# State and output stage of a gated linear attention layer: updates in four row groups, states scaled on ScalarE, low parts on VectorE

## The reference, cut to what matters

```python
b = jnp.cumsum(g, axis=1)
o_inter = q*exp(b) @ S
A = (q k^T with decay exp(b_t - b_s), lower triangle)
o_intra = A @ v
k_dec = k * exp(b_last - b)
S_new = exp(b_last)[..., None] * S + k_dec^T @ v
...
o = o * rsqrt(mean(o*o) + EPS) * head_gain
o = o * silu(r)
return o @ w_out, S
```

## Time and profile before

| | us |
|---|---|
| median of 3 runs | 1556.71 (1556.33 to 1563.7) |
| the profiled execution, its own time | 1557.0 |
| its span in the trace | 1555.2 |
| TensorE busy | 1532.7 |
| VectorE busy | 1106.0 |
| GpSimd busy | 488.5 |
| ScalarE busy | 441.4 |

### The profile page before, as it was taken

The page is one execution under the profiler, slowest core; times in us unless marked ns, Lnnn a source line. Parts: engine busy times, 40 slices in busy tenths (PEclk is TensorE's granted clock), DMA queues, the critical chain, the costliest instruction groups (busy, mean ns, idle before and its releaser), DMA issues.

```text
span 1555.2 us, 25977 instructions
## 1 busy us (share of the span) xinstructions
PE 1532.7 (99%) x10294; PEld 1514.5 (97%) x10294; DVE 1106.0 (71%) x1315; ACT 441.4 (28%) x692; POOL 488.5 (31%) x207
## 2 busy tenths in 40 slices
PE   7999999999999999999999999999999999999997
PEld 6999998899999999999999999999999999999996
DVE  6566665754977777777778645548977787777777
ACT  5355554343212121211215111115221212212123
POOL 2422221143233333323332333332333333233330
PEclk9999999999999999999999999999999999999998
DMA  6211116222222222122222222222222222222212
GB/s 216 80 55 55 55 55 239 90 72 69 68 76 74 68 81 79 57 80 71 78 71 65 92 82 68 82 68 78 66 78 72 77 81 66 68 81 67 77 47 78
DMA packets 34841, 123.76 MB, mean 80 GB/s; under 512 B 3888, under 2 KB 6832, under 8 KB 33616
## 3 DMA queue, kind: packets, MB, share of 16 engines
q1 hardware_dynamic: 31840, 108.37, 22.3%
q10 hardware_dynamic: 2928, 14.35, 2.5%
HBM read 114.48 MB, written 8.22 MB: 79 GB/s over the span
## 4 chain that ended last, share of the span: by engine, by line
PE 94%; DVE 3%; ACT 1%; DMA 1%; DVEq 1%; issue 0%; POOL 0%; SPq 0%; ACTq 0%
PE ps L409 64%; PE ps L425 21%; PE ps L611 2%; PE ps L511 2%; PE ps L710 1%; PE ps L635 1%; PE ps L563 1%; PE ps L525 0%; DVE sq L770 0%; DMA s<-states 0%; DMA raw<-w_units 0%; DVE x L1161 0%; PE ps L645 0%; DVE snew L979 0%; PE ps L492 0%; PE ps L437 0%
## 5 line engine op out<-in xcount | busy, mean ns | idle before, releaser
L355 POOL TENSOR_TENSOR wl<-raw,wh 128x1024 fp32r<-128x1024 f32 x190 | 472.3, 2492 | 966.9 <-ACT wh L1244 927.7
L409 PE MATMUL ps<-xh,wh 128*128 128x260 f32 (+3 forms) x2144 | 494.9, 312 | 0.0
L409 PE MATMUL ps<-xl,wh 128*128 128x260 f32 (+3 forms) x2144 | 493.5, 312 | 0.0
L409 PE MATMUL ps<-xh,wl 128*128 128x260 f32 (+3 forms) x2144 | 493.4, 312 | 0.0
L409 PEld LDWEIGHTS ps<-xl,wh 128*128 128x128 f32 x2144 | 382.5, 189 | 0.0
L409 PEld LDWEIGHTS ps<-xh,wh 128*128 128x128 f32 x2144 | 381.8, 189 | 0.7
L409 PEld LDWEIGHTS ps<-xh,wl 128*128 128x128 f32 x2144 | 382.2, 189 | 0.0
L1244 ACT ACTIVATE wh<-raw 128x1024 fp32r<-128x1024 f32 x196 | 204.2, 1055 | 302.1 <-PE ps L409 276.9
L801 DVE TENSOR_TENSOR x<-ps,x 128x644 f32<-128x644 f32 (+2 forms) x200 | 158.8, 823 | 94.7 <-PE ps L425 67.7
L1013 DVE SCALAR_TENSOR_TENSOR y<-zp,par,y 128x660 f32<-128x660 f32 (+1 forms) x192 | 185.7, 967 | 26.5 <-issue 21.7
L425 PE MATMUL ps<-gl,wh 128*128 128x322 f32 (+1 forms) x768 | 177.2, 312 | 0.0
(11 more groups left out here) (158 smaller groups left out, 1238.6 us busy)
## 6 DMA issues: line engine op xcount, KB each, us to landing
raw<-w_units SPq DMA_DIRECT2D x196, 512.0 KB, 3.5
s<-states ACTq DMA_DIRECT2D x4, 1024.0 KB, 6.0
state_sample<-snew ACTq DMA_DIRECT2D x4, 1024.0 KB, 4.1
x<-x_t SPq DMA_DIRECT2D x8, 328.0 KB, 8.3
x<-x_t ACTq DMA_DIRECT2D x1, 2624.0 KB, 13.1
y_t<-x SPq DMA_DIRECT2D x4, 384.0 KB, 2.4
y_t<-x SPq DMA_DIRECT2D x4, 256.0 KB, 2.2
ffn_last<-zl ACTq DMA_DIRECT2D x2, 396.0 KB, 3.4
```

Source lines behind the costliest of these rows:

```text
L355: pool.tensor_tensor(wl[:, j, :, :], raw[:, j, :, :], wh[:, j, :, :].bitcast(F32), ALU.subtract).then_inc(sem["lo_done"], 1)
L409: mm = pe.matmul(ps[:, p, c:c + z - a], w[:, ring, k, :], v[:, k, a:z], start=(k == 0 and w is wh and v is hi), stop=(k == KT - 1 and w is ...
```

## The change

- TensorE: the tail comes ahead of the samples, and both sample slots are opened before the first of them. The eight sample products run on 32 rows each, in the order of the four row groups, first the even sample of each group, then the odd ones. The groups write four different banks. `kd` has two masked copies of k instead of four (`C_PARITY`).
- States: ScalarE multiplies the eight old states by their decay into `snew` (`scale_states`), for head 0 before the loop, for head h + 1 in head h after the stores. VectorE adds the products in two additions of 128x1024.
- ScalarE in the last head of the stage before: the exponentials t = 6, 7 and 8 come before both Silu steps, and VectorE makes `decayed(h, 7)` and `(h, 8)` before it takes the last r.
- The states of heads 0 and 1 are asked for when TensorE has read tiles 0 to 3 and 0 to 6 of `xh` for the last time (`inputs_used`).
- `ol` is made by VectorE (`low_out`) between the two output scalings of the next head; `split_out` comes after the first square. The table for logarithm and exponential is asked for in the first head norm only. The prompt's last state has two buffers.

```diff
     for h in range(HEADS):
-        s.straight(("U", h, 0), ("U", h, 1), ("U", h, "tail"), ("U", h, 2))
+        s.straight(("U", h, 0), ("U", h, "tail"), ("U", h, 1), ("U", h, 2))
...
-        for k in range(KT):
-            pool.wait_ge(sem["oh_done"], k + 1)
-            pool.tensor_tensor(ol[:, k, :], qk[:, k, :], oh[:, k, :].bitcast(F32),
-                               ALU.subtract).then_inc(sem["o_done"], 1)
...
+                if k in marks:
+                    mm.then_inc(sem["inputs_used"], 1)
...
+            open_slot(("U", h, 1))
+            open_slot(("U", h, 2))
+            for odd in range(2):
+                for group in range(4):
+                    rows = slice(32 * group, 32 * group + 32)
+                    mm, p = update(h, 1 + group // 2, group % 2 * 2 + odd, kd[rows, 5 + odd, :], v_tok[rows, 5, vs])
+                    if odd and group % 2:
+                        mm.then_inc(filled[p], 1)
...
+                early = n == 3 and h == HEADS - 1
+                if early:
+                    dve.drain()
+                    decayed(h, 7)
+                    decayed(h, 8)
                 take_value(kind, h, e)
...
+        def low_out(h):
+
+            for k in (2 * h, 2 * h + 1):
+                dve.wait_ge(sem["oh_done"], k + 1)
+                dve.tensor_tensor(ol[:, k, :], qk[:, k, :], oh[:, k, :].bitcast(F32),
+                                  ALU.subtract).then_inc(sem["o_done"], 1)
...
+            dve.wait_ge(sem["states_scaled"], h + 1)
+            for j in range(2):
+                p = take(("U", h, 1 + j))
+                states = snew[:, h % 2, 4 * j:4 * j + 4, :].rearrange("p s v -> p (s v)")
+                dve.tensor_tensor(states, ps[:, p, :], states, ALU.add).then_inc(freed[p], 1)
...
+                if h and e == 0:
+                    low_out(h - 1)
...
+        def scale_states(h):
+
+            act.wait_ge(s0_in_s[h % 2], 16 * (h // 2 + 1))
+            if h >= 2:
+                act.wait_ge(snew_stored[h % 2], 16)
+            for n in range(SEQS):
+                last = act.activation(snew[:, h % 2, n, :], s0[:, h % 2, n, :], ACT.Copy,
+                                      scale=dec[:, h, 5 + n:6 + n])
+            last.then_inc(sem["states_scaled"], 1)
+
+        for h in range(2):
+            act.wait_ge(sem["inputs_used"], h + 1)
+            load_states(h)
+        gate_r(HEADS - 1, 0)
+        gate_r(HEADS - 1, 1)
+        act.drain()
         take(("r", HEADS - 1, 1))
-        load_states(0)
-        load_states(1)
+        scale_states(0)
...
+            if h + 1 < HEADS:
+                scale_states(h + 1)
             for e in range(2):
...
-            if h:
-                split_out(h - 1)
+                if h and e == 0:
+                    split_out(h - 1)
```

81 lines of the change are left out of this document (33 added, 48 removed).

## The result

The changed kernel takes **1551.47 us** in the median of ten runs (1547.57 to 1552.18). The kernel before, in ten runs of which the three on record above are the first, takes 1559.94 us (1554.62 to 1565.62). The ratio is 0.9948, 95% interval 0.9927 to 0.9968: 0.52% faster, 8.1 us (the medians differ by 8.5). The prediction split its chances almost evenly at 0.5%; the interval lies on both sides of that border, so these runs do not say on which side the change is. The forecast was 8.6 us less. As a time it was 1548.1 us, within its range, but 3.4 us under the median, nearly all of it because the three runs it started from (1556.71) lay 3.2 us under the median of the ten. Between the two profiled executions the difference is 7.0 us (1557.0 and 1550.0).

What follows compares the result with a forecast made beforehand. TensorE bounds the kernel, busy 1532.7 of 1555.2 us. The terms 2.7 + 1.55 + 1.95 + 2.0 + 0.7 - 0.3 = 8.6 us gave a median of 1548.1 us, range 1544.5 to 1555 with rival 1.

Steps and rivals of the forecast that it cites:

- start, to the first T: Start of the rebuilt stage: earlier loads of states let head 0's outputs end at 253.2 instead of 255.94, saving 2.7 us.
- T: The end of a head's output products on TensorE, from which the prediction counts times within the next head.
- head cycles at full clock: Time from one T to the next: 15.15 us, 14.5 in the last head; savings 1.55, 1.95 and 2.0.
- chain lets the norm start: VectorE's chain, not TensorE's updates, sets the head norm's start: T + 4.8 instead of T + 6.4.
- sum of squares: On VectorE ahead of the chain: takes 0.83 us instead of 2.07, as GpSimd no longer works there.
- eight scalings: ScalarE's eight 128x256 activations per head on the states: 0.36 us each, 2.9 us in all.
- samples' 16 records: The samples' products on TensorE in four row groups: half the serial 3.9 us, 2.0; up to 2.3 hidden under the chain.
- ScalarE's charge: ScalarE's second square comes late by 0.1 us at most: 0.1 for each of three heads, 0.3 in all.
- two stretches: TensorE at granted clock 0.50 behind output products of 16 columns, left in the sum; none would give 3.3 us back.
- Rival 1: The row groups don't overlap, updates stay at 6.4 us: 2.05 us saved, 1554.7 in the median; chance 0.13.
- Rival 2: ScalarE becomes the bound, a scaling taking 0.72 us: 5.4 us saved, 1551.3; chance 0.09.
- Rival 3: Slower than before: the clock falls behind each of eight output blocks, six stretches more, 9.8 us, 1557.9; chance 0.05.

Runs made afterwards that it cites:

- b2: Kernel before with the 16-column output products spread between the dense ones and writing their columns three times, nothing of the change: 1558.01 us, ratio 1.001.
- c3: Changed kernel with the 16-column output products both spread between the dense ones and writing their columns three times: 1546.2 us, ratio 0.9942.
- c1_spread: Changed kernel with the 16-column output products spread between the dense ones, order alone: 1545.31 us, ratio 0.9936.
- u2: Changed kernel with the outputs' low parts on GpSimd and the high parts behind the second square again: 1553.48 us, ratio 0.9965.
- u1: Changed kernel with the eight 32-row sample products reordered, both of a row group behind each other: 1550.48 us, ratio 0.9944.
- u2b: Changed kernel with only the outputs' low parts on GpSimd again, high parts where the change puts them: 1549.86 us, ratio 0.9946.
- u3: Changed kernel with the states scaled and added in one step on VectorE again, no scalings on ScalarE: 1550.8 us, ratio 0.9954.
- u4: Changed kernel with the last head's exponentials and the first loads of states where they stood before: 1553.95 us, ratio 0.9965.
- the c kernels: Three changed kernels with edited 16-column output products (spread, wider, or both): 1545.31, 1546.99 and 1546.2 us.
- u5: Changed kernel with the sample products on 64 rows, sample by sample, the tail still ahead: 1556.94 us, ratio 0.9993.
- c2_wide: Changed kernel with each 16-column output product writing its columns three times, width alone: 1546.99 us, ratio 0.9923.
- b1: Kernel before with only the tail-first slot order, the four row groups and their two masks: 1555.99 us, ratio 0.9993.
- a_again: Changed kernel run again with no edit, as reference for u1, u2 and u4: 1550.21 us, ratio 0.9946.

## Why the prediction was right, and where its steps were not

**What came out as worked out.** The gain at equal clock is 8.5 us (1553.4 against 1544.9 at 0.997, with the outputs' order changed), 7.9 (b2 against c3) or 9.4 to 9.8 (the changed kernel against before, 0.992 to 0.995); the sum said 8.6. That the medians differ by 8.5 is in part luck: at equal clock the change brings about 1 us more than the sum, and its lower clock takes about 2 us back. The terms in the profiled runs:

| term | forecast | measured |
|---|---|---|
| start, to the first T | 2.7 | 2.8 (255.94 less 252.63, less 0.49 by which the stage began sooner) |
| head cycles at full clock | 15.15, 15.15, 14.5 | 15.08, 15.44, 14.41 (c3_both); 15.02, 16.49, 14.36 (c1_spread) |
| chain lets the norm start | T + 4.8 | T + 4.71 |
| sum of squares | 0.83 | 0.83 |
| wait at the output projection | gone | gone |
| eight scalings | 2.9 (0.36 each) | 3.30 (0.41 each) |
| samples' 16 records | 2.0 | 1.15 (c1_spread, u2) |

The head norm 4.8 us after T was the step on which everything stood. At full clock it starts at T + 4.70 to 4.73 in the changed kernel and in u1, u2b, u3, u4 and the c kernels, but for two things. In the third head of most builds the gap of 0.43 us stands inside the chain; 0.37 us of it reached the norm in c3, and no row of the chain before showed it. And where ScalarE is late with the states, the chain is too (below). That VectorE's chain, not TensorE's updates, would set it was right too. VectorE's busy time, 14.4 us in the prediction though its parts add to 14.3, is 14.25 in head 1.

**The samples' products were mis-sized.** The forecast took half of the serial 3.9 us, "since each product is two records of one group that stand behind each other". They take 1.15 us. The changed kernel's row has all 26 records; where another wait splits the row, as in c1_spread at 270.62, the 16 stand alone.

u1 shows that the reasoning fails, not only the size: with four records of a group in a row the updates grow by 0.14 us. The serial 3.9 us were right for the old order only (4.0 by the row of before); on 64 rows in the new order the records take 3.0 (u5). The wrong size cost nothing, as anything up to 2.3 us lies under the chain; TensorE waits 1.25 us there instead of the 0.3 foreseen. The Trainium skill (TensorE: Matmul & The Clock Gate, Part 3: Packing small matmuls, Measured speedup vs the span model) has 3.07 times the rate for four groups; here 3.9 serial us against 1.15 is 3.4 times, but part of that is the order's: against u5's 64 rows it is about 2 times (3.0 to 1.4). By that page the estimate of 1.3 us was the better one.

**ScalarE's charge was not due, another was left out.** 0.41 us for a scaling lies between the forecast's 0.36 and its upper end 0.46. At 0.46 the square would have been late by 0.3 us, but c3's three cycles sum to 44.93 us, 0.13 over the 44.8 that stood before the charge, which the gap in the chain explains by itself. The Trainium skill (ScalarE: Activation LUTs, Rules for kernel authors) led to an estimate of 0.51 us each and 4.1 us a head; the trace has 3.30, so the rule overprices this row of eight by a quarter, and the forecast's 1 us later by it did not come.

What the prediction put at nothing, without a reason, is ScalarE's wait for the states of head 2, asked for at the first T. In the six profiled runs where ScalarE waits for them they come 9 to 12 us later. In the changed kernel and in c3 (2.13 and 0.86 us of waiting) TensorE lost nothing by it; in c1_spread it set the chain back by 1.1 us. The states of head 0 have less room than the prediction gave them, too. It let them land by about 244 at no cost; they came at 241.80 in the changed kernel, but at 243.11 in u2 and 243.63 in c2_wide, and there the norm behind the first T stands at T + 5.84 and T + 5.75, 1.1 and 1.0 us late.

**Why the time is not lower.** In the profiled runs 7.0 us arrived of 8.6. By head, the gains are 1.54, 0.61 and 0.93 us, against 1.55, 1.95 and 2.0. Of the 2.4 us missing there, 2.0 are the clock, which the sum left in two stretches, and 0.4 the gap in the third head's chain (0.43 us at 276.65). The sooner beginning of the stage (0.49) and the charge of 0.3 that was not due give some of it back. In the changed kernel it was at half from 264 to 274 us and again around 290:

```profile
262.00:265.00 3.00, 3.00 (x24) 3.00 (x24) 2.85 (x4) 1.38 (x4) 0.00 (x0) 0.82 0.68 279
265.00:268.00 3.00, 3.00 (x15) 2.74 (x13) 0.68 (x2) 3.00 (x7) 0.00 (x0) 0.50 0.02 8
...
271.00:274.00 3.00, 3.00 (x9) 2.46 (x9) 1.65 (x2) 0.72 (x1) 0.00 (x0) 0.50 0.53 164
...
289.00:292.00 3.00, 3.00 (x19) 2.03 (x21) 1.91 (x4) 0.00 (x0) 0.00 (x0) 0.63 0.00 0
```

Head 1 lost 18.47 - 15.15 = 3.3 us to it (what head 1 had lost before), head 2 1.0 of its 1.35 and head 3 1.06. The forecast allowed 3.3 either way, so it lies inside; over all runs the changed kernel's mean clock is 0.9926 against 0.9939, and at about 1.5 us for 0.001 that is 2 us of the gain. The price of a stretch changed as well: at the beginning of a head, half clock now costs through the chain, since VectorE waits for the first group (0.92 us at 274.69), and the norm is 1.0 and 1.1 us late by it in heads 2 and 3, where the updates of before lost 1.6.

**Rivals.** Rival 1, no overlap, fell with the first row of updates; its price of 6.6 us over the forecast is close to what u5 lost in the median (6.7), though only 4 of those are the longer products. Rival 2, ScalarE as the bound, fell with the price of a scaling (0.41 us, not 0.72), but ScalarE did set the pace for 1 us where it waited for states. Rival 3, the clock behind all eight output blocks, came true in part: TensorE does idle more and the clock is a little lower, but by two or three stretches, not six. Its reason, the idle time, is not shown: u5, whose updates leave TensorE no such wait, has a lower clock still (0.9906 in the mean).

**What of the change pays** (differences at equal clock, from few runs each): the place of the high parts, through the sum of squares, 3.4, 3.0 or 1.2 us (u2; none of it is due to the low parts' engine, u2b), the four row groups about 4 us (u5), the states on ScalarE 0 (u3), the early start 0.1 to 1.7 (u4). The order of slots with the tail first was never undone by itself; u5's rows put 0.95 us a head on it where the chain does not bind. Without the earlier sum of squares the groups wait 2.5 us for the chain in the last two heads (b1).

## What to carry to other kernels

When a change shortens the engine that bounds, look at once for what it will wait on next, and work out that time from the other engine's rows: here the groups made TensorE wait for VectorE's chain, and an earlier high part took 1.2 us off that chain in two heads. A load that an engine newly waits for belongs into that sum too, even if it costs nothing in one execution. When GpSimd slows VectorE, first ask when GpSimd runs; moving its trigger by one instruction was worth as much as taking the work from it. And before a forecast of half a per cent, ask how far the runs of one kernel lie apart and why: a median of three was 3.2 us off, and a table by granted clock showed what the medians mixed, though only to 1 or 2 us with so few runs.

## What the runs showed of the hardware

- Products of 32 rows in four row groups overlap even when neighbouring records are of one group: 26 records in 3.46 us in turn, 3.60 us group by group; on 64 rows 5.49 us, and 6.44 us on 64 rows with the tail between the samples. Sixteen records of 32 rows are busy 1.4 us, of 64 rows 3.0 and 4.0.
- Two of GpSimd's subtractions of 128x656 take 3.10 us ahead of VectorE's sum of squares and 3.70 us across it, and the sum goes from 0.83 to 2.06 us.
- VectorE stops for 0.43 us ahead of the third update of the chain in the third head, with no releaser named: so in the changed kernel (276.65), in a_again, u1, u5 and all three c kernels. It moves with the number of instructions ahead of it: in u2 and u2b it stands one instruction later (0.44 us ahead of the tail's update), in u3 0.45 us stand at 267.19, ahead of an output scaling in head 1, and in u4 there is none in this stage. Where it falls into the chain it sits on the path. What it is was not tried.
- A load of 1 MB of states, asked for at 252.82 us while the 2.6 MB reload of the inputs of 245.17 was under way, landed at 263.6 us, 10.8 us later; the page's median of the four loads rose from 6.0 to 7.4 us. That the reload is the cause is not shown. It cost TensorE nothing in the changed kernel's profiled run and 1.1 us in c1_spread's (asked for at 252.63, used at 263.19).
- Runs of the kernel before differ by their mean granted clock from 0.989 to 0.998, and by some 12 us with it (1565.5 us at 0.989, 1553.2 us at 0.998), also on one chip (0.989 to 0.998 in 24 runs). TensorE shows no idle time in the changed kernel's stretches at 0.50 quoted above, and none in the 3 us ahead of the fall at 264 us (busy 3.00 of 3 from 259 to 262 at full clock). What makes it fall in one run and not in the next stays open.
